# A two-layer streaming encoder on one core: attention by query tiles, with the output projection between its units

## The chip, the cores and the metric

The kernel runs on one core of a Trainium2 chip, as one program. A core has five engines with a queue each: TensorE (PE in the profile; its weight loads are PEld), VectorE (DVE), ScalarE (ACT), GpSimd (POOL) and SyncE (SP), which here only issues DMAs. They share an on-chip memory (SBUF, 128 partitions) and eight accumulation banks of 128 x 512 fp32 (PSUM, `ps`). The metric is the time of the whole program in device microseconds, the median of the runs.

## The reference

Two layers over 512 prompt rows and 32 sample rows of width 1024 (544 rows, here five row tiles: four of 128 and one of 32). All is fp32.

```
layer 0:  x = x + pooling_mixer(rms_norm(x));   x = x + hier_moe(rms_norm(x))
layer 1:  h = rms_norm(x)
          q, k, v = split(h @ w_qkv)             # 1024 x 3072, 16 heads of 64
          q, k = rms_norm per head
          s = q @ k.T / 8 + rel_bias;  masked by chunks of 64
          o = softmax(s) @ v                      # prompt: keys 0..i of its own; samples: 128 cached keys + 32
          x = x + o @ w_o                         # the output projection, 1024 x 1024
          x = x + hier_moe(rms_norm(x))
hier_moe: logits = x @ [w_r1 | w_r2] + b;  best group of 4, best 2 of its 8 experts;
          y = sum over both of gate * (silu(x @ w_gate[e]) * (x @ w_up[e])) @ w_down[e]
```

The outputs are the rows after both layers, the pooling states and the new K and V rows.

## The kernel before

The program has one stream of instructions for each engine, ordered by hand and linked by semaphores. The stages of layer 1 matter here.

**The qkv product** takes w_qkv in six pieces of 512 columns. ScalarE copies a piece to fp32r (`split_att`, L809), VectorE subtracts that from the fp32 piece (L1139), and TensorE adds three fp32r products for each 128 rows of depth (`split_product`, L1535 to L1537). The high and low parts lie in the buffer called `pair`.

**The attention** goes over units. A unit is one pair of heads and one tile of 128 queries; the tile i sees the keys of tiles 0 to i, so a unit has 128, 256, 384 or 512 keys. Pairs are the outer loop, tiles the inner: 8 pairs x 4 tiles are 32 prompt units; then come four sample units (four heads of 32 rows each, 160 keys). The work is a pipeline written as one loop on every engine:

```
for t in range(UNITS + 3):          # TensorE
    scores(t)                       # L1906: fp32, into one of two pairs of banks
    p_transposes(t - 2)             # L1932: the weights, transposed into banks 4 and 5
    values(t - 3)                   # L1951: v times the transposed weights, into bank 6 or 7
```

VectorE adds the bias and takes the row minimum of the negative (`biased(t)`, L1461), scales by the reciprocal sum (`scaled(t-1)`, L1470 and L1473) and copies one head's transposed weights out (`pT_out(t-2)`, L1481). ScalarE takes the exp (`weights(t)`, L1067) and copies the other head's (`pT_out(t-2)`, L1078). After the four tiles of a pair, ScalarE copies the pair's output from bank 6 or 7 (in turn) to fp32r (`oT_out`, L1086) and VectorE makes the low part (L1486). POOL fetches the bias table of a pair of heads (L752) and masks its last chunk (L758).

**The output projection** is two more pieces of the same split product (`token_product`), its sample rows packed as high and low part side by side. VectorE adds each result to x (L1515).

**The second router**: per row tile ScalarE squares and takes the root (L797, L798), VectorE normalises (L1133), TensorE transposes (L1552), both copy the transposes out (L863, L1171), TensorE makes the logits (`logits`, L1618), and ACT stores the row for the gathers of the experts (L856). After it comes a long chain of small VectorE operations that finds each expert's rows.

**The experts**: 32 experts, each with gate, up and down weights of 2 MB, in three buffers each: `ring`, `pair` and `third_pair` (down: `ring` and two ends of `qk`). SyncE issues the loads in the order of a hand-written list (L495, L499, L503): the first three experts' as their buffers come free in the stages before, the gate and up of expert b+3 when TensorE is done with gate and up of expert b. TensorE: L1674 and L1675 (gate, up), L1683 and L1684 (down). L1531 is a filler matmul of 128 x 512 on constants that TensorE does while it waits.

## Time and profile before

| | us |
|---|---|
| median of 3 runs (1492.74 to 1496.09) | 1492.85 |
| the profiled execution, its own time | 1495.79 |
| its span, first to last instruction | 1493.8 |
| busy: TensorE (matmul) | 1283.0 (86%) |
| busy: VectorE / ScalarE / GpSimd | 362.0 / 317.9 / 210.0 |
| read and written | 471.07 MB, mean 315 GB/s |

The chain that ended last is 45% DMA and 45% TensorE. A table by stages counts more than these averages, since each stage has another limit. Times in the rows are microseconds from the first instruction, so that a row's start says which stage it belongs to.
### The profile page before, as it was taken

The page shows a single profiled execution, that of the slowest core. Times are in us where ns is not written, and L with a number is a line of the kernel's source. Part 1 is how long each engine was busy: PE and PEld are TensorE (multiplying, and loading weights), DVE is VectorE, ACT ScalarE, POOL GpSimd, SP SyncE. Part 2 cuts the span into 40 slices and gives each one's busy share as a digit, 9 for nine tenths or more (in the row PEclk, how much of TensorE's full clock was granted, in tenths as well). Part 3 has the DMA queues.
Part 4 walks back from the last instruction along what each step waited for, and adds up shares of the span by engine and source line. Part 5 has one row for each costly group of instructions (what it writes and reads, how often), then busy time and mean ns, then how long its engine had stood idle before and what let it go on. Part 6 is the DMA issues. An engine that isn't in the chain of part 4 may idle for free.

```text
span 1493.8 us, 17253 instructions
## 1 busy us (share of the span) xinstructions
PE 1283.0 (86%) x6384; PEld 670.9 (45%) x6384; DVE 362.0 (24%) x740; ACT 317.9 (21%) x648; POOL 210.0 (14%) x341
## 2 busy tenths in 40 slices
PE   8999988888888788999988799999888878878880
PEld 7643333333333333787865577633333333333330
DVE  4721000000000005543447813601100100000013
ACT  4211111111111113433445612211111111111110
POOL 1011111111111112122320000011111111111100
PEclk9999999999999999999999989999999999998996
DMA  9879999999999999132131042899999999999975
GB/s 362 327 302 395 402 398 408 413 407 405 412 406 401 410 413 308 70 113 87 60 110 44 29 169 89 332 371 395 400 410 406 407 409 408 411 411 401 394 327 189
DMA packets 55915, 471.07 MB, mean 315 GB/s; under 512 B 10829, under 2 KB 11981, under 8 KB 30202
## 3 DMA queue, kind: packets, MB, share of 16 engines
q1 hardware_dynamic: 39486, 433.72, 72.4%
q0 software_dynamic: 13584, 27.69, 5.5%
q10 hardware_dynamic: 2796, 8.97, 1.7%
q8 instruction: 35, 0.57, 0.2%
q14 instruction: 14, 0.11, 0.0%
HBM read 458.03 MB, written 28.04 MB: 325 GB/s over the span
## 4 chain that ended last, share of the span: by engine, by line
DMA 45%; PE 45%; DVE 5%; ACT 2%; issue 2%; SPq 1%; POOLq 0%; ACTq 0%; DVEq 0%
DMA pair<-in_moe_w_up 42%; PE ps L1674 16%; PE ps L1535 4%; PE ps L1536 4%; PE ps L1537 4%; PE ps L1683 3%; DMA qk<-yb 2%; PE ps L1606 1%; PE ps L1906 1%; PE ps L1618 1%; PE ps L1951 1%; PE ps L1808 1%; PE ps L1666 1%; PE ps L1932 1%; PE ps L1809 1%
## 5 line engine op out<-in xcount | busy, mean ns | idle before, releaser
L1350 DVE SCALAR_TENSOR_TENSOR nat<-nat,slot_gate,ps 64x512 f32<-64x512 f32 x64 | 47.3, 739 | 686.3 <-ACT nat L943 686.3
L1674 PE MATMUL ps<-ring,xT 128*64 128x512 f32 x352 | 174.7, 655 | 44.7 <-issue 38.9
L1674 PE MATMUL ps<-pair,xT 128*64 128x512 f32 x352 | 174.2, 653 | 44.5 <-DMA pair<-in_moe_w_up 44.5
L1674 PE MATMUL ps<-third_pair,xT 128*64 128x512 f32 x320 | 160.9, 662 | 43.5 <-issue 24.9
L1675 PE MATMUL ps<-ring,xT 128*64 128x512 f32 x352 | 175.2, 656 | 0.0
L1675 PE MATMUL ps<-pair,xT 128*64 128x512 f32 x352 | 174.7, 654 | 0.0
L641 POOL DMA_INDIRECT yb<-nat,scol x64 | 59.2, 925 | 775.4 <-DVE nat L1346 762.9
L943 ACT ACTIVATE nat<-ps 64x512 f32<-64x512 f32 x64 | 38.0, 594 | 611.4 <-PE ps L1675 611.4
L1675 PE MATMUL ps<-third_pair,xT 128*64 128x512 f32 x320 | 161.3, 663 | 0.0
L1683 PE MATMUL ps<-qk,hidT 128*64 128x512 f32 x336 | 153.1, 598 | 1.2 <-ACT hidT L920 1.2
L1684 PE MATMUL ps<-qk,hidT 128*64 128x512 f32 x336 | 153.2, 599 | 0.0
L1674 PEld LDWEIGHTS ps<-ring,xT 128*64 128x64 f32 x352 | 50.8, 150 | 142.3 <-issue 142.0
L1674 PEld LDWEIGHTS ps<-pair,xT 128*64 128x64 f32 x352 | 50.7, 149 | 142.0 <-issue 141.7
L1535 PE MATMUL ps<-w_hi,hT_hi 128*128 128x512 f32 x256 | 103.1, 403 | 5.1 <-DVE hT_lo L1149 2.7
L1674 PEld LDWEIGHTS ps<-third_pair,xT 128*64 128x64 f32 x320 | 46.8, 152 | 134.8 <-issue 134.5
L1536 PE MATMUL ps<-w_hi,hT_lo 128*128 128x512 f32 x256 | 101.4, 396 | 0.0
L1537 PE MATMUL ps<-w_lo,hT_hi 128*128 128x512 f32 x256 | 101.3, 396 | 0.0
L1346 DVE COPY nat<-ps 64x512 f32<-64x512 f32 x64 | 43.7, 682 | 205.0 <-PE ps L1684 205.0
L1666 PEld LDWEIGHTS ps<-cst,nat 64*128 64x128 f32 x512 | 61.2, 200 | 52.2 <-issue 50.3
L626 POOL DMA_INDIRECT nat<-xn,gcol x64 | 62.6, 978 | 125.8 <-DVE gcol L1319 57.0
L1684 PE MATMUL ps<-ring,hidT 128*64 128x512 f32 x176 | 80.1, 598 | 0.0
L1683 PE MATMUL ps<-ring,hidT 128*64 128x512 f32 x176 | 80.1, 598 | 0.0
(212 smaller groups left out, 1743.0 us busy)
## 6 DMA issues: line engine op xcount, KB each, us to landing
qk<-in_moe_w_down SPq DMA_DIRECT2D x42, 2048.0 KB, 39.9
ring<-in_moe_w_gate SPq DMA_DIRECT2D x22, 2048.0 KB, 34.2
ring<-in_moe_w_up SPq DMA_DIRECT2D x22, 2048.0 KB, 38.7
ring<-in_moe_w_down SPq DMA_DIRECT2D x22, 2048.0 KB, 40.4
pair<-in_moe_w_gate SPq DMA_DIRECT2D x22, 2048.0 KB, 34.6
pair<-in_moe_w_up SPq DMA_DIRECT2D x22, 2048.0 KB, 39.1
third_pair<-in_moe_w_gate SPq DMA_DIRECT2D x20, 2048.0 KB, 34.5
third_pair<-in_moe_w_up SPq DMA_DIRECT2D x20, 2048.0 KB, 38.9
```

What stands on the lines that cost most here:

```text
L626: pool.indirect_dma_start(out=xg[v], out_offset=None, in_=xn_dram[l], in_offset=bass.IndirectOffsetOnAxis(ap=gcol[v][:, :], axis=0), bound ...
L641: pool.indirect_dma_start(out=yb_dram[l], out_offset=bass.IndirectOffsetOnAxis(ap=scol[v][:, :], axis=0), in_=yb[v], in_offset=None, bound ...
L1346: V.tensor_copy(yb[v][:, 0:512], ps[0:BLK, Y_BANK, :]).then_inc(y_lo[l], 1)
L1350: return V.scalar_tensor_tensor(out=hidden, in0=silu, scalar=slot_gate[:, bass.ds(j, 1)], in1=ps[0:BLK, GU_BANK, :], op0=ALU.mult, op1=ALU ...
L1535: mm(out, x_hi, w_h, start=start, stop=False)
L1536: mm(out, x_lo, w_h, start=False, stop=False)
L1537: return mm(out, x_hi, w_l, start=False, stop=stop)
L1666: last = nc.tensor.transpose(ps[:, XT_BANK, k * BLK:(k + 1) * BLK], src[:, k, :], ident[0:BLK, 0:BLK])
L1674: mm(ps[BLK:P, GU_BANK, :], rows, gate[:, at], start=(k == 0), stop=(k == KT - 1))
L1675: last = mm(ps[0:BLK, GU_BANK, :], rows, up[:, at], start=(k == 0), stop=(k == KT - 1))
L1683: mm(ps[0:BLK, Y_BANK, :], rows, slot[:, at:at + 512], start=(k == 0), stop=(k == FT - 1))
L1684: last = mm(ps[BLK:P, Y_BANK, :], rows, slot[:, at + 512:at + D], start=(k == 0), stop=(k == FT - 1))
```

## The change

1. **Order of units.** The four sample units come first. Then the prompt units go tile by tile, from the tile with 512 keys down to the one with 128, with the eight pairs inside (`unit`).
2. **One bank for the output.** Four units (four pairs, one tile) fill bank 6; then ScalarE copies it, in fp32, to `oT` (`third_pair`, later `hT_route`). The first values of the next four wait for that copy. There is no low part.
3. **The projection in plain fp32.** w_o is fetched whole (4 MB) into `pair` after the qkv product. A tile's projection is 16 matmuls of 128 x 512 (two halves of eight) into bank 7, two of them at the end of each step from step 16 on, so that the tile of 512 keys goes with steps 16 to 23, that of 384 with 24 to 31, that of 256 with 32 to 39; the last tile's 16 come after the loop. The sample rows' are 32 columns in four column groups, summed by a matmul with the matrix `fold` (steps 8, 11, 13, 15).
4. **Rows of the router.** Tiles are normalised in the order 4, 3, 2, 1, 0, as far as may be while the projection still runs. The transposes and logits of rows 4 to 1 then precede row 0's.
5. **Bias tables** are fetched unit by unit, of the length the unit needs, in three buffers (before: a pair at a time, in two).
6. **Loads of expert weights.** Gate, up and down of expert 0 and down of expert 1 are issued when the last attention output is copied; gate and up of expert 1 after the last product; those of expert 2, as before, after the logits.

The core of the diff:

```diff
+        UNITS = GROUPS + PAIRS * TILES
+        OT_GROUP = 4
+        OT_ALL = 1 + TILES * PAIRS // OT_GROUP
+        def unit(t):
+            u = t - GROUPS
+            return (NT - 1, t) if t < GROUPS else (TILES - 1 - u // PAIRS, u % PAIRS)
...
+        WO_LAG = 4
+        WO_FIRST = GROUPS + PAIRS + WO_LAG
+        WO_A_STEP = 2
+        def product_step(i, n):
+            return WO_FIRST + (TILES - 1 - i) * (2 * KT // WO_A_STEP) + n // WO_A_STEP
+        def sample_product_step(hf):
+            return WO_FIRST - 2 * WO_LAG + hf * WO_LAG + hf
...
                 load_gate(l, 0, 0)
-                if l == 1:
-                    load_down(l, 0, 0)
-                    sp.wait_ge(split_lo, QUARTERS * ATT_PIECES)
                 load_up(l, 0, 0)
+                load_down(l, 0, 0)
                 if l == 0:
-                    load_down(l, 0, 0)
+                    load_gate(l, 1, 1)
+                    load_up(l, 1, 1)
+                    sp.wait_ge(hT_ps, NT)
+                    sp.wait_ge(xn_stored[l], 16 * NT)
+                    load_down(l, 1, 1)
                 else:
-                    sp.wait_ge(quarters_used, QUARTERS * ATT_PIECES)
-                load_gate(l, 1, 1)
-                load_up(l, 1, 1)
-                sp.wait_ge(hT_ps, (2 * l + 1) * NT)
-                sp.wait_ge(xn_stored[l], 16 * NT)
-                load_down(l, 1, 1)
+                    load_down(l, 1, 1)
+                    sp.wait_ge(att_y, 2 * NT)
...
+                    sp.wait_ge(quarters_used, QUARTERS * QKV_PIECES)
+                    sp.dma_start(wo_all, wo).then_inc(wo_in, 16)
...
+            def load_bias(u):
+                t = u + GROUPS
+                i, pr = unit(t)
+                n = unit_keys(t)
+                if u >= BIASES:
+                    pool.wait_ge(s_biased, heads_through(t - BIASES))
+                pool.dma_start(bias_pair[u % BIASES][:, :, 512 - n:512],
+                               bass.AP(tensor=rel_t.tensor, offset=2 * pr * REL_W + 512 - n,
...
+            for u in range(BIASES, PAIRS * TILES):
+                load_bias(u)
+                hide_later_chunk(u - 1)
...
+            def oT_out(t):
+                act.wait_ge(o_ps, t + 1)
+                i, pr = unit(t)
+                if t < GROUPS:
+                    act.activation(oT[:, :, S:T], ps[:, OT_BANK, 0:PAIRS * SS].rearrange(
+                        "p (c t) -> p c t", c=PAIRS)[:, :, ::-1], ACT.Copy).then_inc(oT_sb, 1)
+                else:
+                    act.activation(oT[:, pr + 1 - OT_GROUP:pr + 1, tok(i)], ps[:, OT_BANK, :].rearrange(
+                        "p (c t) -> p c t", c=OT_GROUP)[:, :, ::-1], ACT.Copy).then_inc(oT_sb, 1)
...
+            early_squares(1)
+            act.wait_ge(act_own, own[0])
+            act.activation(std[:, 3, 1:NT], ssq[:, 3, 1:NT], ACT.Sqrt, bias=const("eps"),
+                           scale=1.0 / D).then_inc(std_ready, NT - 1)
+            for i in range(NT - 1, 0, -1):
+                store_row(1, i)
+            row_squares(1, 0)
+            for i in range(NT - 1, 0, -1):
+                first_chunks(1, i)
+            store_row(1, 0)
+            first_chunks(1, 0)
...
+            def add_product(i, hf):
+                n = ROWS[i]
+                dve.wait_ge(att_y, 2 * turn(3, i) + hf + 1)
+                half = slice(hf * 512, (hf + 1) * 512)
+                V.tensor_tensor(x[0:n, i, half], x[0:n, i, half], ps[0:n, WO_BANK, :],
+                                ALU.add).then_inc(x_mixed[1] if hf == 1 else x_half, 1)
...
+            add_product(1, 1)
+            dve.wait_ge(std_ready, 4 * NT - 1)
+            dve.wait_ge(ffn_gain_in, 32)
+            link(V.reciprocal(rstd[:, 3, 1:NT], std[:, 3, 1:NT]))
+            for i in range(NT - 1, 1, -1):
+                scaled_rows(3, i, route_row(i), ffn_gain)
+            add_product(0, 0)
+            scaled_rows(3, 1, route_row(1), ffn_gain)
+            add_product(0, 1)
+            last_chunks(1, NT - 1)
+            row_normalised(1, 0)
...
+                    if pr % OT_GROUP == 0:
+                        pe.wait_ge(oT_sb, oT_before(t))
+                    at = pr % OT_GROUP * P
                     for k in range(i + 1):
...
+            def product_free(i, hf):
+                if hf == 1:
+                    pe.wait_ge(x_half, turn(3, i) + 1)
+                elif i < NT - 1:
+                    pe.wait_ge(x_mixed[1], turn(3, i))
+            def sample_product(hf):
+                if hf == 0:
+                    pe.wait_ge(wo_in, 16)
+                    pe.wait_ge(oT_sb, 1)
+                product_free(NT - 1, hf)
+                half = slice(hf * 512, (hf + 1) * 512)
+                for k in range(KT):
+                    at = k % HEADS_A_GROUP * SS
+                    last = mm(ps[at:at + SS, WO_BANK, :], oT[:, k, S:T], wo_all[:, k, half],
+                              start=(k < HEADS_A_GROUP), stop=(k >= KT - HEADS_A_GROUP))
+                last.then_inc(stack_ps, 1)
+            def sample_fold(hf):
+                pe.wait_ge(stack_sb, QKV_PIECES + hf + 1)
+                mm(ps[0:SS, WO_BANK, :], const("fold"), wo_stacked, start=True, stop=True).then_inc(att_y, 1)
+            def tile_product(i, first, n):
+                for m in range(first, first + n):
+                    hf, k = divmod(m, KT)
+                    if m == 0:
+                        pe.wait_ge(oT_sb, 1 + (TILES - i) * PAIRS // OT_GROUP)
+                    if k == 0:
+                        product_free(i, hf)
+                    last = mm(ps[:, WO_BANK, :], oT[:, k, tok(i)], wo_all[:, k, hf * 512:(hf + 1) * 512],
+                              start=(k == 0), stop=(k == KT - 1))
+                    if k == KT - 1:
+                        last.then_inc(att_y, 1)
+            for t in range(UNITS + 4):
                 if t < UNITS:
                     scores(t)
                 if 0 <= t - 2 < UNITS:
                     p_transposes(t - 2)
                 if 0 <= t - 3 < UNITS:
                     values(t - 3)
-            pe.wait_ge(oT_sb, OT_ALL)
-            def sum_free(m):
-                if m >= RAW_BANKS:
-                    pe.wait_ge(*((x_half, m - RAW_BANKS + 1) if m - RAW_BANKS < NT else
-                                 (x_mixed[1], m - RAW_BANKS + 1 - NT)))
-            for hf in range(2):
-                token_product(QKV_PIECES + hf, hf * NT, sum_free, att_y)
+                for hf in range(2):
+                    if t == sample_product_step(hf):
+                        sample_product(hf)
+                    if t == sample_product_step(hf) + 3 - hf:
+                        sample_fold(hf)
+                for i in range(1, TILES):
+                    n = (t - product_step(i, 0)) * WO_A_STEP
+                    if 0 <= n < 2 * KT:
+                        tile_product(i, n, WO_A_STEP)
+            tile_product(0, 0, 2 * KT)
```

**TensorE in the middle of the attention.** Here a step of the program before: scores of a unit of 256 keys (`qk`), transposes of one of 512 (`cst,ring`), values of one of 384 (`ring,nat`). In brackets stand the semaphores a row waits for.

```order
L1906 MATMUL ps<-qk 128x256 [waits s_biased]
L1906 MATMUL ps<-qk 128x256
L1932 MATMUL ps<-cst,ring 128x128 [waits p_scaled,pT_second,pT_first]
L1932 MATMUL ps<-cst,ring 128x128 x3
L1932 MATMUL ps<-cst,ring 128x128 [waits p_scaled]
L1932 MATMUL ps<-cst,ring 128x128 x3
L1951 MATMUL ps<-ring,nat 64x128 [waits pT_second,pT_first]
L1951 MATMUL ps<-ring,nat 64x128 x5
```

And the change, the step 19 (384 keys) and the head of step 20; the product is `pair,third_pair`.

```order
L1967 MATMUL ps<-qk 128x256 [waits s_biased]
L1967 MATMUL ps<-qk 128x256
L1967 MATMUL ps<-qk 128x128 x2
L1994 MATMUL ps<-cst,ring 128x128 [waits p_scaled,pT_second,pT_first]
L1994 MATMUL ps<-cst,ring 128x128 x2
L1994 MATMUL ps<-cst,ring 128x128 [waits p_scaled]
L1994 MATMUL ps<-cst,ring 128x128 x2
L2010 MATMUL ps<-ring,nat 64x128 [waits oT_sb,pT_second,pT_first]
L2010 MATMUL ps<-ring,nat 64x128 x5
L2058 MATMUL ps<-pair,third_pair 128x512 x2
L1967 MATMUL ps<-qk 128x256 [waits s_biased]
L1967 MATMUL ps<-qk 128x256
```

The product stands behind the values and before the next scores, and the values at the start of each group of four wait for `oT_sb`, ScalarE's copy.

**ScalarE at the copy of the attention output.** Before, a pair's last steps: exps (`ring<-ring`), transposed weights (`ring<-ps`), the copy (`hT_hi<-ps`).

```order
L1067 ACTIVATE ring<-ring 128x384 [waits s_biased] x2
L1078 ACTIVATE ring<-ps 128x128 [waits o_ps,pT_ps]
L1067 ACTIVATE ring<-ring 128x512 [waits s_biased] x2
L1078 ACTIVATE ring<-ps 128x256 [waits o_ps,pT_ps]
L1086 ACTIVATE hT_hi<-ps 128x512 [waits o_ps]
L1067 ACTIVATE ring<-ring 128x128 [waits s_biased] x2
L1078 ACTIVATE ring<-ps 128x384 [waits o_ps,pT_ps]
```

The change, steps 18 to 20; the copy is `third_pair<-ps`.

```order
L1091 ACTIVATE ring<-ring 128x384 [waits s_biased] x2
L1102 ACTIVATE ring<-ps 128x384 [waits o_ps,pT_ps]
L1091 ACTIVATE ring<-ring 128x384 [waits s_biased] x2
L1102 ACTIVATE ring<-ps 128x384 [waits o_ps,pT_ps]
L1115 ACTIVATE third_pair<-ps 128x4x128 [waits o_ps]
L1091 ACTIVATE ring<-ring 128x256 [waits s_biased] x2
L1102 ACTIVATE ring<-ps 128x384 [waits o_ps,pT_ps]
```

The copy stands at the same place, behind the exps and the copy of transposed weights of its step; what waits for it has moved (before, only values two pairs later, and VectorE's low part).

## Rows read from the trace of the kernel before

**Rows 1.** Table by stretches: busy time (instructions) of each engine, granted clock, DMA share, GB/s
```profile
770.20:875.40 105.20, 83.77 (x810) 60.59 (x809) 75.02 (x282) 59.70 (x189) 6.76 (x15) 0.94 0.13 42
875.40:929.10 53.70, 53.70 (x225) 42.34 (x226) 11.42 (x15) 9.63 (x14) 0.00 (x0) 0.95 0.40 157
929.10:947.00 17.90, 15.80 (x125) 13.79 (x123) 11.56 (x19) 7.94 (x15) 1.84 (x2) 1.00 0.93 357
...
1060.00:1460.00 400.00, 332.06 (x1475) 134.34 (x1473) 36.16 (x51) 53.87 (x100) 53.59 (x94) 0.92 0.98 395
```
**Rows 2.** Chain of waits, from 1060 us: start us, us, what
```profile
1060.27 41.08 DMA pair<-in_moe_w_up
```
**Rows 3.** Timeline, SyncE's DMA issues: start us, us, queue, line
```profile
976.69 0.33 SPq L495 DMA_DIRECT2D ring<-in_moe_w_gate  x1
```
**Rows 4.** Timeline, ScalarE between the qkv product and the attention
```profile
771.31 1.04 ACT L809 ACTIVATE w_hi<-ring 128x1024 fp32r<-128x1024 f32 x1
772.37 1.28 ACT L1067 ACT_TABLE_LOAD   x1
```
**Rows 5.** Timeline, two neighbouring units in the attention, TensorE and ScalarE
```profile
804.72 1.06 PE L1932 MATMUL ps<-cst,ring 128*128 128x128 f32 x8 [1.04 <-DVE ring L1481]
...
805.72 0.88 PE L1951 MATMUL ps<-ring,nat 128*64 128x128 f32 x12
...
807.74 1.09 PE L1951 MATMUL ps<-ring,nat 128*64 128x128 f32 x16
...
808.77 1.13 PE L1906 MATMUL ps<-qk 64*128 64x256 f32 x8
...
810.68 0.72 ACT L1067 ACTIVATE ring<-ring 128x512 f32<-128x512 f32 x1 [1.12 <-DVE ring L1461]
...
812.11 0.36 ACT L1078 ACTIVATE ring<-ps 128x256 f32<-128x256 f32 x1
812.37 0.58 ACT L1086 ACTIVATE hT_hi<-ps 128x512 fp32r<-128x512 f32 x1
```
**Rows 6.** Timeline, TensorE's filler of plain fp32 before the qkv product
```profile
569.32 15.72 PE L1531 MATMUL ps<-cst 128*128 128x512 f32 x36
```
**Rows 7.** Timeline, TensorE in the sample units: scores, then values
```profile
861.03 0.44 PE L1915 MATMUL ps<-ring,qk 64*32 64x128 f32 x8
...
863.65 0.30 PE L1962 MATMUL ps<-ring 128*64 128x32 f32 x2
...
863.89 0.30 PE L1963 MATMUL ps<-ring,nat 32*64 32x32 f32 x2
...
869.15 0.42 PE L1963 MATMUL ps<-ring,nat 32*64 32x32 f32 x2
...
869.50 0.42 PE L1962 MATMUL ps<-ring 128*64 128x32 f32 x2
```
**Rows 8.** Groups by shape, 791.72 to 856 us: busy us, mean ns, idle before
```profile
L1067 ACT ACTIVATE ring<-ring 128x384 f32<-128x384 f32 x12 | 7.3, 607 | 9.2 <-DVE ring L1461 9.2
L1461 DVE CUSTOM_DVE_ANT_0 ring<-ps,ring 128x512 f32<-128x512 f32 x12 | 7.8, 689 | 2.9 <-PE ps L1906 2.9
...
L1481 DVE COPY ring<-ps 128x512 f32<-128x512 f32 x6 | 4.2, 692 | 0.0
```
**Rows 9.** Timeline, POOL: a bias table is fetched and masked
```profile
800.62 0.72 POOL L752 DMA_DIRECT2D ring<-in_rel_bias_reversed  x1 [6.73 <-DVE ring L1461]
804.75 0.20 POOL L758 MEMSET ring<- 64x128 f32 x1 [3.41 <-DMA ring<-in_rel_bias_reversed]
```
**Rows 10.** Timeline, TensorE: last two tiles' logits, then the filler behind them
```profile
943.43 3.58 PE L1618 MATMUL ps<-rw,third_pair 128*128 128x104 f32 x32
946.93 1.55 PE L1531 MATMUL ps<-cst 128*128 128x512 f32 x3
```
**Rows 11.** Table by stretches: the granted clock in two pieces of 2 us
```profile
776.00:778.00 2.00, 2.00 (x9) 1.19 (x8) 1.50 (x8) 1.47 (x5) 0.00 (x0) 0.50 0.00 0
868.00:870.00 2.00, 2.00 (x12) 1.33 (x12) 0.00 (x0) 0.42 (x2) 0.00 (x0) 0.50 0.00 0
```

More of the change, by code:

```diff
@@ L578, in _ @@
                 if l == 0:
-                    for j in range(ATT_PIECES):
+                    for j in range(QKV_PIECES):
                         if j < 2:
@@ L1839, in first_product, with token_product @@
                 token_quarter(early, early, QUARTERS - 1).then_inc(quarters_used, 1)
[L1841 removed]
+            def token_product(piece, between):
+                m0 = piece * NT
                 sample = NT - 1
@@ L1861, in token_product @@
                     last = token_quarter(m0 + i, i, q)
-                    last.then_inc(done if i < sample - 1 else quarters_used, 1)
+                    last.then_inc(raw_ps if i < sample - 1 else quarters_used, 1)
             def raw_free(m):
```

307 lines of the change are left out of this document (144 added, 163 removed).

## The prediction

> **What bounds the kernel now.** I read the table by stages first [rows 1]. The kernel is a row of stages, and the change touches three of them: the attention units (770.2 to 875.4 us), the output projection (875.4 to 929.1) and the second router's rows and logits (929.1 to 947.0). Then come the routing and the second layer's experts. From 1060 us on the DMA share is 0.98 and the chain of waits jumps from one transfer of expert weights to the next [rows 2]: there the transfers set the pace, and TensorE waits. Four things follow from the issues on SyncE's queue [rows 3]. Three experts' weights (nine pieces of 2 MB) can be fetched ahead. The tenth piece, the gate of expert 3, is issued at 976.69, when TensorE has finished gate and up of expert 0. From there 87 pieces follow without a gap. So the end of the program moves by what that issue moves, and that moves with the end of the logits, unless the first nine pieces come late. Everything below is therefore one question: when do the last logits end, against 946.9 us now [rows 10]?
>
> In the attention stage nothing is full: VectorE is busy 75 of 105 us, TensorE 84 [rows 1]. In the projection stage TensorE is busy all 53.7 us. The change puts the second stage's work into the gaps of the first. I name the loop's passes "steps": in step t TensorE does the scores of unit t, the transposes of t-2, the values of t-3, and after the change a piece of product.
>
> **What is removed.** The split of wo into high and low parts on ScalarE and VectorE; of it only the last quarter lies on the path, at the start [rows 4]: ScalarE's L809 of 1.04 us, after which VectorE subtracts and only then takes its first bias. The 53.7 us stage goes. The low parts of the attention output (L1486, 0.69 us, eight) leave VectorE.
>
> **What a step costs TensorE.** From the start of one group to the start of the next [rows 5]: eight transposes 1.00 us (804.72 to 805.72), the values of 512 keys, 16 records, 1.03 (807.74 to 808.77), of which about 0.15 is the gap of a wait. The scores of 512 keys have the same number of columns in all. I take 1.0 for each of the three operations at 512 keys, 0.8 at 384, 0.59 at 256, 0.38 at 128. Eight units of each size: what is left from step 7 on is 20.0 (512 keys, less what steps 4 to 6 did) + 19.4 + 14.2 + 9.1 = 62.7 us.
>
> **What the product costs.** It is plain fp32 in 128x512 matmuls. TensorE's filler matmuls have just this shape: 36 records in 15.72 us, two records a matmul [rows 6], so 0.86 each (0.857 by the spacing of 0.43 a record). A split product needs three records at 0.23 (the 53.7 us are 224 of them and a slow start). So the projection gets dearer on TensorE: 64 matmuls, 54.8 us. 48 of them go into steps 16 to 39, two a step, 41.1 us.
>
> The sample rows: 16 matmuls of 32 columns in four column groups. The nearest row is four heads' scores of 32 rows, eight records of 128 columns in 0.44 us [rows 7]; one after another they would need 0.86, so the groups overlap. I take 2 x 1.71 for the products and 2 x 0.86 for the folds: 5.1 us. The upper end, no overlap, is 16 x 0.86 = 13.7 for the products. The Trainium skill (TensorE: Matmul & The Clock Gate, Part 3 and its closing table) gives three column groups of 32 columns a gain of 2.38, not 3. By that the products would cost some 1.0 more, an estimate from the page, and the forecast would be 1495.8; the row above shows 0.44 for what in a row would be 0.86, with its own latency in it, and does not decide it.
>
> **The new wait.** Before, the output of a pair went to one of two PSUM banks in turn. Now four units share bank 6, and it is the only one: the first values of each next four wait for ScalarE's copy of the last four. The order on ScalarE puts that copy behind the two exps and the pT copy of the same step, and those exps wait for VectorE's bias of scores which TensorE has only just made. At 512 keys, from the end of the scores (808.77 + 1.13 = 809.90) the first exp starts at 810.68, both take until 812.11 [rows 5]; then a pT copy of 512 (0.49 by the spacing), the output copy 0.58 and 0.1 to reach TensorE: 3.38 us. TensorE would have started its values 0.92 after the scores. So it stands 2.46 us. With the shorter exps at fewer keys (0.61 each at 384 [rows 8]) it is 2.2 at 384 keys, 1.97 at 256, 1.73 at 128. There are eight such steps (7, 11, ... 35), two of each: 16.8 us. Behind the waiting values in TensorE's queue are the product piece and the next scores, so VectorE and ScalarE wait too. Nothing hides it, since the product stands behind it and not before it.
>
> **Other pieces.** The additions to x (512 columns like the copy of 0.69 [rows 8]) stand at the head of a VectorE step; VectorE has room in a product step (about 2.5 of 4.1 us at 384 keys). Where there is no product, VectorE is the limit: bias 2 x 0.69, a copy of 0.69 [rows 8], and between them a reciprocal and two scalings, about 1.1 in all, 3.1 to 3.2 against TensorE's 3.0; I add 1.5 us for those steps. The bias tables are now fetched a unit at a time, 32 issues on POOL: an issue takes 0.72 us and lands and is masked 4.1 us after it began [rows 9], and it has three steps, over 8 us: hidden. wo (4 MB) is issued at 770 and is needed some 25 us later: hidden. On SyncE's queue it stands before the expert weights, which now wait for the last attention output and, for expert 1, for the last product.
>
> **The sum,** on TensorE from the end of the qkv product (770.2):
> - to the first values of the samples, 5.0: the last v copy (771.4), a table load of 1.28 [rows 4], then exp, scaling, transposes and copies of the first unit one after another, to 775.2;
> - steps 3 to 6, in which the samples' values (32 matmuls) and the first long units mix. Eight values matmuls take 1.84 us at 2.4 GHz, 2.8 at 1.2 (the spacings 0.23 and 0.35 in [rows 7]). With the rest of these steps 12.3 us at the high level, 20.2 at the low one. The granted clock was low (0.50) in 776 to 778, just after such a pause, and low in 868 to 870 although TensorE was busy with just these matmuls [rows 11]. I take the middle, 16.3, and keep both ends;
> - steps 7 to 39: 62.7 + 41.1 + 5.1 + 16.8 + 1.5 = 127.2;
> - the last tile's product, uncovered: 2 x 6.86 and twice 0.85, since bank 7 is the only one and each half waits for VectorE's addition of 0.69 and two semaphores: 15.4;
> - rows and logits: four of the five rows are done early. TensorE then needs 5 x 1.75 for the logits [rows 10] and 1.0 a tile for the transposes (eight of them, as in [rows 5]), 13.8, and stands about 0.9 for the first copy of a transposed row: 14.7 instead of the 17.9 of [rows 1].
>
> Together 178.6, so the logits end at 948.8, 1.9 us later than 946.9. The stretch from the qkv product to the last product takes 163.9 us in place of 158.9, and the rows and logits give 3.2 back: what the gaps take in, the waits, the dearer product and the uncovered last tile cost again. The expert weights: four pieces (8.4 MB at 395 GB/s, 21 us [rows 1]) are issued about 15 us before the product's end, the rest by 20 us after it; the ninth piece lands as now, some 17 us after the logits, just when the first gather runs. I count nothing for it. The profiled execution took 1495.79 us (span 1493.8); the median of three is 1492.85, 2.9 lower. So the forecast is 1497.7 for such an execution and **1494.8 us** for the median: no change that a measurement of this kernel could tell (about 0.3%, 4.5 us). Its own range, from the ends of steps 3 to 6 (4 us each way) and some 4 us of unseen gaps: 1488 to 1503.
>
> **Rivals.**
> - Slower: the sample products' column groups do not overlap, because stationary tiles of 32 columns at full depth (128 rows) are nowhere in this trace; only 64-row ones are [rows 7]. Price 13.7 - 3.4 = 10.3 us, on the path since the steps around are TensorE's already: 1505.1. It decides as soon as each of the 16 costs 0.16 us more than I took. Chance 0.12.
> - Slower: the eight pauses and the mixed steps keep the clock at 1.2 GHz. For it: [rows 11]. Against it: the attention stage ran at 0.94 in all with TensorE idle a fifth of the time [rows 1]. If steps 7 to 15 (about 39 us, some 30 of it TensorE's own) ran at half speed, it would be about 28 us more: 1523. The Trainium skill (TensorE: Matmul & The Clock Gate, "A second HAM failure mode") warns of such micro-pauses between groups of one bank and the next. Chance 0.06.
> - Faster: ScalarE's copy comes early enough and the waits of 16.8 us shrink to nothing: 1478. Against it: the order of ScalarE's instructions. For it: the wait was never seen; before, two banks covered it. If a third of it is gone and the clock is high in steps 3 to 6, it is about 1485. Chance 0.22 for the two together.
> - The interleaving does not happen as written (a product piece waits for a late output or addition, so the work stays in a row): 929 + 4 = 1497 and up. Chance 0.05.
>
> The forecast has the rest, 0.55. **The numbers:** the range 1478 to 1507 leaves out the clock case and the far ends. Faster by over 0.3%: 0.27 (the faster rival and the low edge of the forecast). Slower: 0.33 (0.23 of rivals and 0.10 from the forecast's upper edge). Within: 0.40.
>
> **What would show it.** In the profile after: the product (a third_pair and pair operand) at 0.43 us a record; TensorE waiting eight times for the output copy, 1.7 to 2.5 us each, before the values; the end of the last product near 934; logits' end near 949 and the gate of expert 3 issued about 30 us later. Sample product groups of 1.7 us, not 6.9. If the values' waits are under 1 us, or the gate of expert 3 is issued more than 5 us from 978.6, the prediction is wrong.

## The result, and the profile after

The changed kernel took 1519.99 us (median of four runs, 1513.95 to 1521.23), the kernel before on the same chip 1494.47 (1492.74 to 1498.58). The ratio is 1.0159, with a 95% interval of 1.0123 to 1.0194: 25 us slower, where no measurable change was forecast, and outside the range. The profiled execution took 1513.95 us (span 1512.0), the fastest of the four, so the rows below account for some 18 us of the 25.

The table by stretches, changed kernel. Columns as in [rows 1]: the granted clock is the number after the busy times.

```profile
775.00:785.00 10.00, 10.00 (x50) 7.17 (x52) 2.40 (x10) 2.67 (x10) 0.97 (x2) 0.50 1.03 417
785.00:795.00 10.00, 10.00 (x50) 6.96 (x48) 5.38 (x15) 3.84 (x11) 2.15 (x4) 0.50 0.38 145
795.00:805.00 10.00, 8.60 (x46) 6.24 (x46) 3.10 (x8) 2.27 (x6) 1.07 (x2) 0.50 0.23 88
805.00:838.60 33.60, 28.38 (x278) 19.00 (x276) 23.11 (x65) 16.91 (x44) 8.01 (x16) 1.00 0.33 99
838.61:936.97 98.36, 88.34 (x457) 43.76 (x456) 40.00 (x171) 34.60 (x116) 16.28 (x35) 0.95 0.18 42
936.97:952.87 15.90, 14.25 (x34) 5.92 (x33) 6.41 (x7) 1.45 (x3) 0.00 (x0) 1.00 1.00 421
952.87:966.81 13.94, 13.57 (x122) 13.18 (x121) 5.48 (x10) 5.18 (x9) 1.84 (x2) 1.00 1.02 431
...
1060.00:1460.00 400.00, 336.77 (x1500) 135.70 (x1500) 35.42 (x51) 54.20 (x101) 56.23 (x98) 0.92 1.01 408
```

Against [rows 1]: the qkv product ends at 770.2 in both. The attention with the product in it now lasts to 952.87, that is 182.7 us, where attention and projection took 158.9 and the forecast said 163.9. Rows and logits take 13.94 in place of 17.9. From 1060 us on the stage is as before, bound by its transfers. Two numbers strike one at once: the clock of 0.50 for 30 us, from 775 to 805, and the 0.95 of the long stretch behind.

The waits of TensorE from 800 to 953 us, changed kernel: who waits for whom, us in total, times, the longest.

```profile
PE ps L2010 <- ACT third_pair L1115: 14.6, 7, 2.5
PE ps L2058 <- DVE x L1549: 1.8, 3, 0.9
PE ps L2010 <- DVE ring L1542: 1.4, 1, 1.4
```

L2010 are the values, L1115 is ScalarE's copy of the attention output: the new wait stands there seven times. The eighth (step 7) is put down to VectorE's copy of transposed weights, 1.4 us. Together 16.0, forecast 16.8.

The timeline of the changed kernel, in places. Columns: start us, us, engine, line, what, count, and in brackets the idle time before it.

```profile
778.34 2.08 PE L1967 MATMUL ps<-qk 64*128 64x256 f32 x8
780.35 0.69 PE L1994 MATMUL ps<-cst,ring 128*128 128x128 f32 x2
780.96 0.42 PE L2020 MATMUL ps<-ring 128*64 128x32 f32 x2
...
817.61 0.72 ACT L1091 ACTIVATE ring<-ring 128x512 f32<-128x512 f32 x1 [1.41 <-DVE ring L1522]
818.34 0.71 ACT L1091 ACTIVATE ring<-ring 128x512 f32<-128x512 f32 x1
819.04 0.58 ACT L1102 ACTIVATE ring<-ps 128x512 f32<-128x512 f32 x1
819.52 0.58 ACT L1115 ACTIVATE third_pair<-ps 128x512 f32<-128x512 f32 x1
820.25 1.09 PE L2010 MATMUL ps<-ring,nat 128*64 128x128 f32 x16 [2.49 <-ACT third_pair L1115]
...
828.31 1.92 PE L2041 MATMUL ps<-pair,third_pair 128*32 128x512 f32 x16
...
855.72 1.03 PE L2010 MATMUL ps<-ring,nat 128*64 128x128 f32 x12 [2.25 <-ACT third_pair L1115]
856.68 3.47 PE L2058 MATMUL ps<-pair,third_pair 128*128 128x512 f32 x4
860.09 0.70 PE L1967 MATMUL ps<-qk 64*128 64x256 f32 x4
...
996.77 0.33 SPq L521 DMA_DIRECT2D ring<-in_moe_w_gate  x1
```

Four things are to be read here. At 778 us the eight records of scores take 2.08 us (1.13 in [rows 5]) and a pair of sample values 0.42, the slow form of [rows 7]. At 817 to 820 the chain behind the wait is just the forecast one: exp, exp, the copy of transposed weights, the copy of the output, then the values. At 856.68 the four records of product that follow such a wait take 3.4 us to the next scores instead of 1.9. And the gate of expert 3 is issued at 996.77, 20.1 us later than in [rows 3]; from there to the end it is 515 us, as before 517. So the theory of what sets the end held: the program ends later by what the logits end later.

The clock at that place, changed kernel, in pieces of 2 us:

```profile
852.00:854.00 2.00, 1.47 (x14) 1.07 (x12) 1.16 (x6) 0.59 (x2) 0.00 (x0) 1.00 0.18 49
854.00:856.00 2.00, 0.28 (x6) 0.31 (x8) 1.20 (x3) 1.58 (x6) 0.95 (x2) 1.00 0.16 25
856.00:858.00 2.00, 2.00 (x14) 1.16 (x10) 0.00 (x0) 0.00 (x0) 0.00 (x0) 0.58 0.50 115
858.00:860.00 2.00, 2.00 (x3) 0.38 (x2) 0.00 (x0) 0.00 (x0) 0.00 (x0) 0.57 0.00 0
860.00:862.00 2.00, 2.00 (x19) 1.42 (x20) 1.72 (x7) 0.60 (x3) 0.00 (x0) 1.00 0.00 0
```

TensorE stands for 2.25 us, starts again, and the granted clock falls to the lower of its two levels for some 3 us, when the product is what runs: in pieces of 1 us it is 0.50 from 857 to 859. I call this a dip. It happened behind three of the eight waits (856, 876, 910 us).

### The profile page after: what moved, and what is told of

It reads as the page before. It is cut to its first block and busy times, and to the rows that moved or that the text cites. A ratio compares the mean times of both kernels' runs of the same rounds, so it can differ in the third digit from the quotient of the medians.

```text
span 1512.0 us, 17138 instructions
## 1 busy us (share of the span) xinstructions
PE 1304.0 (86%) x6320; PEld 657.6 (43%) x6320; DVE 348.1 (23%) x719; ACT 309.1 (20%) x637; POOL 234.5 (16%) x389
## 5 line engine op out<-in xcount | busy, mean ns | idle before, releaser
L1735 PE MATMUL ps<-ring,xT 128*64 128x512 f32 x352 | 176.7, 660 | 48.6 <-issue 41.8
L1735 PE MATMUL ps<-third_pair,xT 128*64 128x512 f32 x320 | 157.2, 649 | 42.1 <-issue 25.3
L1736 PE MATMUL ps<-ring,xT 128*64 128x512 f32 x352 | 177.1, 662 | 0.0
L965 ACT ACTIVATE nat<-ps 64x512 f32<-64x512 f32 x64 | 38.1, 596 | 609.5 <-PE ps L1736 609.5
L1736 PE MATMUL ps<-third_pair,xT 128*64 128x512 f32 x320 | 157.5, 650 | 0.0
L1596 PE MATMUL ps<-w_hi,hT_hi 128*128 128x512 f32 x192 | 77.2, 402 | 4.1 <-DVE hT_lo L1204 2.7
L950 ACT ACTIVATE nat<-ps 64x512 f32<-64x512 f32 x64 | 38.1, 595 | 197.4 <-PE ps L1745 197.4
L1744 PEld LDWEIGHTS ps<-qk,hidT 128*64 128x64 f32 x336 | 42.5, 136 | 75.7 <-issue 73.0
```

The lines of the kernel that those rows point to most:

```text
L950: act.activation(yb[v][:, 512:D], ps[BLK:P, Y_BANK, :], ACT.Copy).then_inc(y_hi[l], 1)
L1596: mm(out, x_hi, w_h, start=start, stop=False)
L1735: mm(ps[BLK:P, GU_BANK, :], rows, gate[:, at], start=(k == 0), stop=(k == KT - 1))
L1736: last = mm(ps[0:BLK, GU_BANK, :], rows, up[:, at], start=(k == 0), stop=(k == KT - 1))
L1744: mm(ps[0:BLK, Y_BANK, :], rows, slot[:, at:at + 512], start=(k == 0), stop=(k == FT - 1))
```

## The experiments

To compare profiles I use one stretch throughout: from the first scores, those of step 0 (in the changed kernel 770.21), to the end of the last product, since what lies before it moves by up to 5 us from one execution to another. Ratios are to runs of the kernel before, taken beside them on the same chip; its medians there were 1496.8 to 1497.0. In all of them the theory on trial is that two misjudged costs, the waits with what follows them and the low clock, make the loss.

| kernel | time, us | ratio [95%] | stretch, us |
|---|---|---|---|
| before | 1494.47 | 1 | 158.9 |
| changed | 1519.99 | 1.0159 [1.0123, 1.0194] | 182.7 |
| e0_after_again | 1521.18 | 1.0152 [1.0129, 1.0175] | 185.8 |
| e1_copy_first | 1495.16 | 0.9987 [0.9972, 1.0002] | 160.5 |
| e2_product_ahead | 1501.94 | 1.0023 [1.0005, 1.0040] | 165.3 |
| e3_fillers | 1512.73 | 1.0095 [1.0067, 1.0123] | 173.5 |
| e4_four_a_step | 1498.14 | 1.0001 [0.9985, 1.0017] | 162.7 |
| e5_first_and_fill | 1490.19 | 0.9942 [0.9906, 0.9978] | 155.6 |
| e6_product_last | 1520.28 | 1.0158 [1.0114, 1.0202] | 185.0 |
| e7_first_ahead_fill | 1480.35 | 0.9901 [0.9869, 0.9932] | 146.5 |
| e8_first_product_last | 1506.23 | 1.0076 [1.0051, 1.0102] | 171.8 |
| e9_more_fillers | 1485.46 | 0.9933 [0.9912, 0.9953] | 150.7 |
| e10_best_again | 1485.48 | 0.9923 [0.9896, 0.9951] | 146.5 |

**The changed kernel again** (no edit).

> The changed kernel once more, unchanged. Its first profile took 1512.0 us of span, its other runs 1518 to 1519. Three theories for the 18 to 25 us it lost. Wait: TensorE stands eight times, 17 us in all, for ScalarE's copy of the output. Clock: TensorE ran at the low level from 775 to 805 us and again for some 3 us after three of those waits. Product: a record of the product costs 0.48 us in its short groups, not 0.43, and it is uncovered in the last tile. All three expect again about 1.016 times the kernel before (1514 to 1521 us). If the spread among its runs is the clock's, a longer run has a longer low stretch between 775 and 940 us; by the wait or the product theory the attention takes the same time in both and the difference lies elsewhere.

The loss repeats. In this profile the half clock stood behind more of the waits, and the stretch is 3.1 us longer than in the first (step 27 has a dip there, 896.24 to 903.61 against 890.96 to 896.76): the size of that cost differs between executions.

**The copy first.** ScalarE copies the finished output before the exps of its step, not behind them.

```diff
             for t in range(UNITS + 4):
+                if t - 4 == GROUPS - 1 or (...):
+                    oT_out(t - 4)
                 if t < UNITS:
                     weights(t)
...
                 if 0 <= t - 2 < UNITS:
                     pT_out(t - 2)
-                if t - 4 == GROUPS - 1 or (...):
-                    oT_out(t - 4)
```

> ScalarE's copy of the attention output moves to the head of its step, ahead of the two exps and the copy of the transposed weights. Wait theory: the eight waits of TensorE (17 us together) vanish, and the dips of the clock behind three of them (4.8 us) with them: 17 to 22 us less than the changed kernel, 1495 to 1500. If the dips come from something else, 17 less. Rival: the next wait takes its place (the exps are 0.6 us later, so VectorE's scaling and TensorE's transposes are late), then less than 10. Product theory: a product record still costs 0.48.

Of TensorE's waits from 800 to 936 us that of the last tiles' halves for VectorE's addition is left, as in the changed kernel:

```profile
PE ps L2058 <- DVE x L1549: 1.8, 3, 0.9
```

and the table by stretches shows no dip behind 830 us (TensorE busy 20.0 of 20.0 us, clock 1.00), but still the low clock ahead:

```profile
785.00:795.00 10.00, 10.00 (x51) 7.15 (x50) 3.56 (x13) 3.67 (x12) 2.02 (x4) 0.50 0.75 288
...
850.00:870.00 20.00, 20.00 (x123) 10.44 (x121) 11.53 (x43) 7.82 (x26) 4.75 (x10) 1.00 0.26 64
```

One instruction at another place in ScalarE's order gives back 26 us. Against the first profile of the changed kernel the stretch is 22.2 shorter: 16.0 of waits, 5.1 of dips (below), 0.8 in step 8, which ran partly at the low clock, and 0.3 not assigned. Against the profile of e0_after_again, which had one dip more, it is 25.3 shorter. The faster rival of the prediction had a kernel without these waits at 1478; with them gone it takes 1495, so the interleaved form then only draws level with the kernel before.

**The product ahead of the values.** TensorE does its piece of product between transposes and values, so that it runs while ScalarE comes to its copy.

```diff
                     p_transposes(t - 2)
+                for i in range(1, TILES):
+                    ...
+                        tile_product(i, n, WO_A_STEP)
                 if 0 <= t - 3 < UNITS:
                     values(t - 3)
...
-                for i in range(1, TILES):
-                    ...
-                        tile_product(i, n, WO_A_STEP)
```

> The two product matmuls of a step stand ahead of the values, behind the transposes. Wait theory: in the five steps with both a wait and a product (19, 23, 27, 31, 35) the product covers 1.9 of the 2.25 to 1.8 us, the three waits of steps 7, 11 and 15 stay: about 9 us less than the changed kernel. Clock theory: the dips behind the waits of steps 19, 23 and 31 are gone too, 4.8 more, 14 in all. If the wait was not on the path, nothing changes.

TensorE's waits are 7.2 us in total for the attention output and the copy beside it (14.6 + 1.4 before), mainly those of steps 7, 11 and 15, where there is no product to cover them; and behind 830 us the clock is 1.00 in every stretch:

```profile
PE ps L2010 <- ACT third_pair L1115: 5.8, 5, 2.5
PE ps L2010 <- DVE ring L1542: 1.4, 1, 1.4
...
830.00:860.00 30.00, 27.23 (x222) 16.91 (x221) 17.71 (x58) 14.36 (x40) 6.65 (x14) 1.00 0.33 89
```

The stretch is 17.4 shorter, more than the 14 expected: 8.8 of waits, 5.1 of dips, and some 4 that I had not expected, because a step with a product takes 0.2 us less in this order (4.18 in place of 4.38 at 384 keys; see the run with all three edits). The dips went although ScalarE's copy came as late as before: TensorE worked in the meantime, and what was left of the wait was 0.5 us or less.

**Three fillers in the pause.** Three 128x512 matmuls before the first unit's transposes, where TensorE had stood 2.1 us for VectorE.

```diff
+                if t == 2:
+                    keep_busy(3, WO_BANK, ident, some)
                 if 0 <= t - 2 < UNITS:
                     p_transposes(t - 2)
```

> Three filler matmuls of 128x512 on constants in the pause of 2.1 us between the first scores and the first transposes of the samples, nothing else. If the pause at 772 us is what lowers the clock, it stays at the high level through the first steps: steps 3 to 8 take 21 us in place of 33, so 10 us less than the changed kernel. If it is the samples' own narrow matmuls that do it, the clock falls all the same, a few us later at best: 0 to 3 us less. The waits and the product are as in the changed kernel.

The table by stretches of this run:

```profile
775.00:785.00 10.00, 9.60 (x113) 6.28 (x106) 3.94 (x20) 5.83 (x18) 1.05 (x2) 1.00 0.93 326
...
795.00:805.00 10.00, 8.00 (x80) 5.25 (x80) 5.79 (x17) 3.86 (x11) 1.99 (x4) 1.00 0.44 154
805.00:830.00 25.00, 21.88 (x208) 15.30 (x206) 17.57 (x50) 12.92 (x34) 6.25 (x12) 0.93 0.31 87
```

The clock is full where it had been at half, with the DMA engines as busy as there (0.93 against 1.03 from 775 to 785 us, w_o above all), so their load is not what lowers it. The kernel is 8.5 us faster than the changed kernel run beside it. From the scores of step 0 to those of step 9 it is 28.2 us (774.79 to 803.00) instead of 38.9 (770.21 to 809.07), the time of the fillers included. TensorE's waits stay (12.1 us for the copy of the output, 4.7 for VectorE's copy beside it, 16.8 in all), and so do dips behind them, 0.93 from 805 to 830 us.

**Four matmuls in every other step** (on top of the copy first).

```diff
-        WO_A_STEP = 2
+        WO_A_STEP = 4
-            return WO_FIRST + (TILES - 1 - i) * (2 * KT // WO_A_STEP) + n // WO_A_STEP
+            return WO_FIRST + (TILES - 1 - i) * PAIRS + 2 * n // WO_A_STEP
...
-                    n = (t - product_step(i, 0)) * WO_A_STEP
-                    if 0 <= n < 2 * KT:
+                    n = (t - product_step(i, 0)) * WO_A_STEP // 2
+                    if 0 <= n < 2 * KT and n % WO_A_STEP == 0:
```

> Edit: the copy of the attention output heads ScalarE's step (as in e1_copy_first, 1495.2 us, 0.9987 of the kernel before), and the product goes four matmuls into every other step in place of two into every step; the same matmuls in all. Theory short groups: a group of product between attention matmuls pays some 0.2 us once, whatever its length (two matmuls took 1.92 us to the next scores, 1.71 by the spacing of a long run). Then 12 groups instead of 24 save about 2.5 us: 1492.7, ratio 0.997. Theory by the record: each record is dearer there (0.48 us in place of 0.44), so nothing changes: 1495, 0.9987. Theory starved steps: steps without a product fall back to VectorE's pace of 2.7 us at 384 keys against some 2.4 on TensorE, 12 steps by some 0.3: 3.6 us slower before any saving, 1496 to 1499.

At 384 keys the steps 16 and 17 take 8.56 us, against 8.76 with two matmuls in each: a group costs 0.2 once, as the first theory had it. But the steps 18 and 19 take 9.06, since the transposes wait 0.45 us for ScalarE's copy of transposed weights (L1102), and at 128 keys two steps take 6.43 (896.13 to 902.56) instead of 6.14, with a wait of 0.41 for the same copy. So the third theory had the starved steps, with ScalarE as the engine that is waited for and not VectorE. In the profiles the stretch is 2.2 us longer than in e1_copy_first; the two times are not told apart.

**Copy first and fillers.** Both edits above.

> Edit: the copy heads ScalarE's step, and three filler matmuls of 128x512 in plain fp32 run on TensorE in its pause before the first unit's transposes (as in e3_fillers). Theory the two costs are separate (26 us for the waits and what follows them, 8.5 us for the low clock in steps 3 to 8): 1495.2 - 8.5 = 1486.7, about 0.993 of the kernel before, granted clock 1.00 throughout the attention, gate of expert 3 issued near 971. Rival, the gain of the fillers was partly the same time as the first waits (steps 7 and 11), which ScalarE and VectorE set and not TensorE: only 4 to 5 us, 1490 to 1491.

1490.2, but its six runs lie between 1478.9 and 1494.0. The profile shows one reason, in the table by stretches:

```profile
775.00:780.00 5.00, 4.92 (x43) 3.06 (x43) 1.80 (x10) 2.40 (x12) 0.00 (x0) 0.97 0.91 339
780.00:785.00 5.00, 5.00 (x28) 3.34 (x24) 1.69 (x6) 1.83 (x6) 0.96 (x2) 0.50 1.03 417
785.00:795.00 10.00, 10.00 (x53) 7.06 (x53) 4.74 (x15) 3.60 (x11) 1.94 (x4) 0.58 0.55 207
```

TensorE had been busy for 4.92 of the 5 us before, and the clock fell all the same, in the sample units with their values of 32 columns. So a pause is not the only thing that lets it fall here. The median is the number that the rival gave, but by luck: steps 4 to 6 took 16.1 us here, mostly at the low clock, and 10.5 in e7_first_ahead_fill, where it stayed high. Without that fall this profile would have been some 5.6 us shorter, by an estimate from these two numbers.

**The product last.** All 64 matmuls of the tiles come after the loop, with their additions and squares behind.

```diff
-                for i in range(1, TILES):
-                    ...
-                        tile_product(i, n, WO_A_STEP)
-            tile_product(0, 0, 2 * KT)
+            for i in range(TILES - 1, -1, -1):
+                tile_product(i, 0, 2 * KT)
```

> Edit: the changed kernel, but all 64 matmuls of the tiles' product come after the loop, tile by tile, with their additions and squares behind; the rows and logits are otherwise as in the changed kernel. Waits for ScalarE's copy stay. Theory the interleaving fills real gaps: without a product the steps 16 to 39 run at VectorE's pace (about 53 us) plus the waits (some 12), and the product of 48 matmuls takes 41.1 us and six times 0.85 for the one bank, together 111 against 98.4 measured in the changed kernel: about 12 us slower, 1532. Rival, what the interleaving hides it pays back in half-clock stretches behind the waits and in short groups (11 us): between 1518 and 1523.

The time is that of the changed kernel, in the range of the rival (1518 to 1523) and not at my 1532. What the interleaving hides it gives back. The timeline of this run shows how little there was to fill:

```profile
844.00 0.92 PE L1963 MATMUL ps<-qk 64*128 64x256 f32 x8
845.10 0.85 PE L1990 MATMUL ps<-cst,ring 128*128 128x128 f32 x6 [0.17 <-ACT ring L1102]
845.87 0.88 PE L2006 MATMUL ps<-ring,nat 128*64 128x128 f32 x12
846.68 0.92 PE L1963 MATMUL ps<-qk 64*128 64x256 f32 x8
```

A step of 384 keys without a product lasts 2.46 to 2.68 us and TensorE is busy in nearly all of it. VectorE's pace of 2.7, which I had expected to bind, was an estimate too high.

**The product last, the copy first.**

> Edit: the copy heads ScalarE's step (as in e1_copy_first), and all 64 matmuls of the tiles' product come after the loop (as in e6_product_last). Theory few gaps: in e6_product_last a step without a product lasts 2.46 us at 384 keys, 1.8 to 2.2 at 256 and 1.2 to 2.1 at 128, TensorE's own pace, so that an interleaved matmul costs almost as much as one in a row; against e1_copy_first (1495.2) the product in a row then costs only six more waits for the one bank, 0.86 each, and some 2 us of gaps at 128 and 256 keys: about 1502, ratio 1.004. Rival, VectorE's pace (2.7, 2.2, 1.7 us a step) was hidden in e6_product_last by the waits: 14 us behind e1_copy_first, 1509.

1506.2, between the two theories (1502 and 1509), 11 us behind e1_copy_first. This is what the interleaving is worth when nothing waits for the copy. In the profile the loop's steps 16 to 39 hold 6.7 us of idle TensorE in all, mostly transposes that wait for ScalarE's copy L1102, 5.6 us of it in the steps of 128 keys; the one bank costs 5.7 us of waits instead of 1.8; and the clock was 0.85 from 860 to 880 us. With the waits present (e6 against the changed kernel) the same rearrangement is worth nothing measurable. TensorE's waits in those steps tell why. In e8_first_product_last (831 to 878 us):

```profile
PE ps L1990 <- ACT ring L1102: 5.8, 9, 1.6
PE ps L1990 <- DVE ring L1540: 0.6, 1, 0.6
```

and in e6_product_last (841 to 894 us):

```profile
PE ps L2006 <- ACT third_pair L1115: 8.5, 5, 2.1
PE ps L1990 <- ACT ring L1102: 1.5, 5, 0.5
```

While TensorE stands for the output copy, ScalarE and VectorE catch up, and 5 us of the other gaps are gone. So a wait costs less than its length where there are gaps, and in full where a product has filled them: for the copy's place e6 pays 14 us against e8, the changed kernel 25 to 26 against e1_copy_first. In the profiles steps 7 to 15 pay 7.2 us of it in both pairs; steps 16 to 39 pay 6.0 in e6, and 15.0 in the changed kernel, where 5.1 are dips.

**All three edits: copy first, product ahead, fillers.**

> Edit: all three, the copy at the head of ScalarE's step, the product ahead of the values in TensorE's, three fillers in the pause. Theory: once the copy is early nothing waits before the values, so the place of the product changes nothing and this is e5_first_and_fill again, 1486.7. Rival: the values still wait some tenths for ScalarE's and VectorE's copies of the transposed weights (0.15 us a step in the kernel before), and the product hides that in 24 steps: 3 us less, 1483 to 1484.

1480.35 us, 0.9901 [0.9869, 0.9932]: faster than both kernels. The clock stayed high in the sample units this time:

```profile
775.00:785.00 10.00, 9.92 (x87) 6.81 (x85) 4.65 (x21) 4.42 (x18) 0.96 (x2) 1.00 0.98 384
```

The timeline of one of its steps:

```profile
822.60 0.92 PE L1967 MATMUL ps<-qk 64*128 64x256 f32 x8
823.46 0.88 PE L1994 MATMUL ps<-cst,ring 128*128 128x128 f32 x6
824.17 1.88 PE L2058 MATMUL ps<-pair,third_pair 128*128 128x512 f32 x4
825.98 0.88 PE L2010 MATMUL ps<-ring,nat 128*64 128x128 f32 x12
826.78 0.92 PE L1967 MATMUL ps<-qk 64*128 64x256 f32 x8
```

A step takes 4.18 us. With the copy first and the product behind the values it took 4.38 (835.43 to 839.81 in e1_copy_first), without a wait in either. Against e5_first_and_fill the stretch is 9.1 us shorter, 5.6 of it the clock in steps 4 to 6. The rest is the 3 us of the rival, but they did not come through a hidden wait as it said: TensorE loses less when the 128-row product stands between transposes and values than when it stands before the scores of 64 rows: 1.81 us to the next group in place of 1.92, and 0.71 in place of 0.81 for the transposes. Why, no run here shows.

**More fillers, and the best version again.** One filler more behind the values of each sample unit; beside it all three edits unchanged.

```diff
                     values(t - 3)
+                if 0 <= t - 3 < GROUPS:
+                    keep_busy(1, WO_BANK, ident, some)
```

> Edit: e7_first_ahead_fill (1480.4, runs from 1477.9 to 1487.7) with one more filler matmul of 128x512 behind the values of each of the four sample units, 3.4 us of added work on TensorE. In the profile of e5_first_and_fill the clock fell at 780 us without a pause before it, in the values of 32 columns; in that of e7_first_ahead_fill it did not fall. Theory the narrow matmuls can let the clock fall by themselves, in part of the executions, at some 6 us each time: with fillers among them it stays at 1.00 in all, the time is 1481 to 1482 and its spread shrinks to 2 or 3 us. Rival, the spread comes from elsewhere: the time rises by the 3.4 us, to 1484, with the spread of e7_first_ahead_fill.

> Edit: none against e7_first_ahead_fill (copy first, product ahead of the values, three fillers in the pause), to stand beside e9_more_fillers on the same chip. If the clock at 780 us is what parts its executions, the times fall in two groups, near 1478 and near 1485; the ratio should again be near 0.990.

1485.46 (1483.6 to 1491.6) against 1485.48 (1479.4 to 1490.0). Both profiled executions had the clock at 1.00 from 775 to 960 us; the four fillers show in the stretch with 4.2 us. The medians are equal, the spread is a little smaller with more fillers and not two or three us, and of the ten times of e10 four lie from 1479.4 to 1481.7 and six from 1485.3 to 1490.0, which is no more than a hint of two groups. Neither theory is borne out: that the medians are equal although the fillers add 4.2 us may mean that they gave something back in other executions, but within this spread that is not shown. What moves these executions by 10 us goes with the clock of TensorE as a whole: over the whole program the mean granted clock is 0.942 to 0.944 in the four executions of e10 below 1482 us, and 0.935 to 0.940 in the six above 1485. At which place it was lower stays open, since each run has only one profile. Over its two runs the best version stands at 0.990 and 0.992 of the kernel before.

## Why the prediction was wrong

It was wrong by 25 us in the median, and by 16.3 against the profiled execution (1513.95, forecast 1497.7). In the profile the gate of expert 3 is 18.2 us behind the forecast 978.6. Term by term:

- **What bounds the kernel: right.** The last logits' end sets the issue of the tenth piece, and that sets the end; 20.1 us later there, 18.2 more in the span.
- **Start, 5.0:** 5.3 (775.54). **The wait, 16.8:** right in place, number and size, 16.0, and of the forecast lengths (2.46, 2.2, 1.97, 1.73) each was met within 0.05: 2.49 at 820, 2.25 at 856, 2.01 at 876, 1.78 at 910. Only that of step 7 was 1.40, behind transposes at the low clock. What I left out is what a wait does next.
- **Steps 3 to 6, 16.3 (12.3 or 20.2): the first step that failed.** I took the middle between the two clocks, and it was the low end: 20.4. What misled me was that the clock of the kernel before recovers in about 3 us from the pause at this place (3.05 us there, 2.07 here); the table of the kernel before shows it:

```profile
775.00:777.00 2.00, 2.00 (x12) 1.35 (x10) 1.93 (x10) 1.67 (x7) 0.00 (x0) 0.50 0.02 8
777.00:779.00 2.00, 2.00 (x14) 1.00 (x12) 1.32 (x6) 0.68 (x4) 0.00 (x0) 0.75 0.00 0
779.00:781.00 2.00, 0.72 (x10) 0.51 (x7) 1.96 (x9) 1.77 (x6) 0.74 (x1) 1.00 0.00 0
```

  There prompt units followed, here sample units with their narrow matmuls, and the clock stayed at 0.50 for 30 us. That the narrow matmuls kept it there is likely but not shown: no run has the new kernel with other units first. It reached past step 6 too: without the wait, steps 7 and 8 took 4.1 us more than the sum had for them.
- **Steps 7 to 39, 127.2:** 141.1 in all. Beyond those 4.1, the **dips behind the waits** were missing altogether. Steps 19, 23 and 31 took 8.35, 7.09 and 5.93 us; the same steps of e1_copy_first (4.38, 3.72, 3.07) and the wait of each make 6.63, 5.73 and 4.85: 4.2 us. Steps 24 and 32 began at the low clock and took 0.9 more. So the dips cost 5.1 us in this profile, and there is one more in that of e0.
- **The product, 41.1:** sized by the spacing of a long run of one matmul, 0.43 a record. In groups of two between attention matmuls it takes 1.92 a group and not 1.71. With the last two groups in a row that is 4.7 us more in the 24 steps; the attention part of these steps was 0.5 longer than the sum had it.
- **The last tile, 15.4:** 15.9. **Rows and logits, 14.7:** 13.9. **Sample products:** 1.86 us for eight matmuls of 32 columns in four column groups, near the forecast 1.71, and not 6.9. Expert weights and bias tables cost nothing, as forecast.

Start 0.3, steps 3 to 6 4.1, steps 7 and 8 4.1, steps 9 to 15 0.3, dips 5.1, product and step 5.2, last tile 0.5, less 0.8 each for the waits and for the logits: the 18.0 by which the logits end late (966.8 against 948.8). So some 13 of the 18 are TensorE's clock, and 5 the size of a product group. The slower rival named that cause and gave it 1523, by steps 7 to 15 at half speed. That the time came near this is partly luck, since the place was another (steps 3 to 8, and the product behind the waits); its chance of 0.06 was too small. For it spoke [rows 11], which I had read and then set at the middle of two levels. The page it named (the Trainium skill, TensorE: Matmul & The Clock Gate, "A second HAM failure mode") says that TensorE's short idle times between groups can make the clock swing between its two levels, and that the loss is in the time between bursts. This case's trace agrees on the swing: full, 0.58 and full again around 857 us. It does not agree on the place of the loss, which is here in the burst itself: the four records of product behind the wait took 3.4 us in place of 1.9. The 2.38 of the Trainium skill for three column groups (the same page, Part 3) is not tested by the four groups here, which gain 6.9 / 1.86 = 3.7.

The deeper fault was in the argument on gaps. The attention stage had TensorE idle for a fifth of its time, and I let the product fill it; but at 384 and 256 keys TensorE itself all but sets the pace, and in the steps that took the product only 6.7 us were to be had (e8), while each of the 24 groups cost 0.2 of its own. The sum did not show this fault, since it counted TensorE's own work. The waits for the copy stood in front of the product piece, not beside it, and cost 11 us more than with the product last: just what the interleaving brings where there are none.

The loss beyond the profiled execution, 6 us in the median, is not explained by rows: e0's profile shows more dips and is the slowest of its runs, the first profile shows fewer and is the fastest, which fits. The mean granted clock of the whole program fits too: 0.933 in the profiled execution, 0.927 to 0.929 in the other three. More there is not.

## What to carry to other kernels

When several units share an output bank in place of two in turn, look where the copy that frees it stands in the copying engine's queue: here its place behind two exps cost 26 us, and at the head of the step nothing. Put independent matmuls ahead of the operation that may wait, not behind it: they hide the wait, and they keep TensorE's clock. And before you fill "idle" time, read the idle time of just those steps that will take the filling: an average over the stage promised 21 us, the steps held 6.7.

## What the runs showed of the hardware

- The granted clock fell to 0.50 after a pause of 2.1 us and stayed there for some 30 us while sample units ran, in all seven profiles that have this pause. With three filler matmuls in it the clock stayed at 1.00 (e3, e7, e9, e10) or fell 5 us later without any pause (e5). The same edit in the same place gave both.
- Behind a wait of 1.8 to 2.5 us the clock was near 0.58 for about 3 us in three cases of eight, and in four of eight in the second profile of the same kernel. With the product ahead, which left 0.5 us or less of these waits, it was 1.00 behind all five (e2).
- A plain fp32 matmul of 128x512 costs 0.88 us in a row in the product (16 records from 945.80 to 952.87), 0.96 in pairs ahead of scores of 64 rows, 0.905 in pairs ahead of values of 128 rows.
- Eight fp32 matmuls of 32 columns at full depth, spread over four column groups, take 1.86 us, about the time of two of the product's.
